# Where sixteen retention projection units stand among the RWKV-7 steps of a hybrid layer

## The reference

```python
def ab_mixer(h, pos, shift_prev, S_rwkv0, S_ret0, p, i):
    z = h @ p['ab_w_in'][i]
    za, zb = z[..., :A_SHIFT_COLS], z[..., A_SHIFT_COLS:]      # RWKV 1792, retention 2048 columns
    zs = za + (za_prev - za) * p['rwkv_mu'][i]
    ...                                                        # r, k, v, decay, a, gate, kk
    # per token: S = S*w - (S kk)(kk*a)^T + v k^T ;  o = S r
    o_a, S_rwkv = rwkv7_recurrence(r_h, decay, k_h, v_h, kk, a_h, S_rwkv0)
    o_a = (group_norm(o_a, ...) + sum(r_h * k_h * r_k) * v_h) * gate
    qr, kr, vr, gr = split(zb)                                 # 4 heads of 128 each
    qr = rotary(qr, pos); kr = rotary(kr, pos) * DK_B ** -0.5
    o_b, S_ret = retention_chunked(qr, kr, vr, S_ret0)
    o_b = group_norm(o_b, ...) * silu(gr)
    return concatenate([o_a, o_b], -1) @ p['ab_w_out'][i], ...
```

## Time and profile before

| what | value |
|---|---|
| median of three runs | 1522.76 us |
| the profiled execution | 1519.87 us, span 1518.1 us |
| TensorE matmul | 1421.7 us busy, 94% of the span |
| VectorE / ScalarE / GpSimd | 908.3 (60%) / 645.1 (42%) / 445.8 (29%) |
| mean granted TensorE clock | 0.97 |

### The profile page before, as it was taken

One profiled execution on the slowest core, in us unless ns is written; L12 is line 12 of the kernel. 1 busy time (PEld: TensorE's weight loads), 2 busy tenths in 40 slices (PEclk: granted clock), 3 DMA queues, 4 the chain that ended last, 5 costly groups with the idle time before them and its releaser, 6 DMA issues.

```text
span 1518.1 us, 30482 instructions
## 1 busy us (share of the span) xinstructions
PE 1421.7 (94%) x12028; PEld 1342.7 (88%) x12028; DVE 908.3 (60%) x1211; ACT 645.1 (42%) x975; POOL 445.8 (29%) x455
## 2 busy tenths in 40 slices
PE   7999999877998799999999999998998889999996
PEld 7999998866598589999999999987987769999996
DVE  4444456975464366555567776557777657655554
ACT  4333336533042434433443443366685444434333
POOL 3333132532221321112411114530006652111343
PEclk9999999999699799999999999999998999999998
DMA  7555543300053054555435555433434014455541
GB/s 277 166 165 186 171 130 98 109 6 30 22 177 98 21 180 139 164 158 186 164 118 164 159 163 182 164 92 119 134 133 153 30 71 167 140 165 165 187 156 51
DMA packets 50621, 203.37 MB, mean 134 GB/s; under 512 B 5696, under 2 KB 5696, under 8 KB 49760
## 3 DMA queue, kind: packets, MB, share of 16 engines
q1 hardware_dynamic: 46224, 181.03, 37.3%
q0 software_dynamic: 4016, 19.81, 3.6%
q10 hardware_dynamic: 288, 1.18, 0.2%
HBM read 192.17 MB, written 9.83 MB: 133 GB/s over the span
## 4 chain that ended last, share of the span: by engine, by line
PE 79%; DVE 11%; ACT 5%; issue 3%; POOL 1%; DMA 0%; ACTq 0%; POOLq 0%; DVEq 0%
PE gemm L2436 22%; PE gemm L2440 22%; PE gemm L2437 21%; DVE wlo L2388 3%; ACT whi L2383 2%; PE job L707 1%; PE gemm L2463 1%; PE job L739 1%; DVE M L1975 1%; PE gemm L513 1%; PE job L831 1%; PE job L1629 0%; PE job L1582 0%; PE job L1652 0%; PE job L849 0%
## 5 line engine op out<-in xcount | busy, mean ns | idle before, releaser
L2436 PE MATMUL gemm<-xhi,whi 128*128 128x290 f32 (+1 forms) x2040 | 619.9, 304 | 28.3 <-DVE wlo L2388 23.2
L2388 DVE TENSOR_TENSOR wlo<-raw,whi 128x1024 fp32r<-128x1024 f32 (+1 forms) x319 | 434.1, 1361 | 316.1 <-ACT whi L2383 313.8
L2383 ACT ACTIVATE whi<-raw 128x1024 fp32r<-128x1024 f32 (+1 forms) x319 | 358.5, 1124 | 607.3 <-PE gemm L2440 603.9
L2440 PE MATMUL gemm<-xlo,whi 128*128 128x290 f32 (+1 forms) x2040 | 610.5, 299 | 4.0 <-DVE xlo L400 4.0
L2437 PE MATMUL gemm<-xhi,wlo 128*128 128x290 f32 (+1 forms) x2040 | 607.6, 298 | 0.0
L2436 PEld LDWEIGHTS gemm<-xhi,whi 128*128 128x128 f32 x2040 | 389.5, 191 | 43.9 <-DVE wlo L2388 26.2
L2440 PEld LDWEIGHTS gemm<-xlo,whi 128*128 128x128 f32 x2040 | 388.4, 190 | 5.4 <-DVE xlo L400 4.7
L2437 PEld LDWEIGHTS gemm<-xhi,wlo 128*128 128x128 f32 x2040 | 389.6, 191 | 2.1
L2436 PE MATMUL gemm<-hhi,whi 128*128 128x288 f32 x704 | 209.6, 298 | 2.5 <-POOL hlo L2985 1.8
L2437 PE MATMUL gemm<-hhi,wlo 128*128 128x288 f32 x704 | 209.8, 298 | 0.0
L2440 PE MATMUL gemm<-hlo,whi 128*128 128x288 f32 x704 | 209.1, 297 | 0.0
(11 more groups left out here) (434 smaller groups left out, 1518.3 us busy)
## 6 DMA issues: line engine op xcount, KB each, us to landing
raw<-in_w_dram SPq DMA_DIRECT2D x255, 512.0 KB, 3.5
raw<-in_w_dram SPq DMA_DIRECT2D x64, 704.0 KB, 4.0
M<-in_ret_in_dram POOLq DMA_DIRECT2D x1, 2048.0 KB, 9.0
out_ret_s_dram<-M POOLq DMA_DIRECT2D x1, 2048.0 KB, 8.1
s_space<-in_gdn_in_dram POOLq DMA_DIRECT2D x4, 512.0 KB, 5.1
M<-in_gdn_in_dram POOLq DMA_DIRECT2D x4, 512.0 KB, 5.4
out_gdn_s_dram<-s_space POOLq DMA_DIRECT2D x4, 512.0 KB, 4.2
out_gdn_s_dram<-M POOLq DMA_DIRECT2D x4, 512.0 KB, 6.3
```

Of the source, the lines that this page charges most:

```text
L2383: nc.scalar.activation(whi[c % SPL][:, 0:w], raw[c % RAW][:, 0:w], ACT.Copy).then_inc(hi_ready, 1)
L2388: nc.vector.tensor_tensor(wlo[c % SPL][:, 0:w], raw[c % RAW][:, 0:w], whi[c % SPL][:, 0:w].bitcast(F32), ALU.subtract).then_inc(lo_ready, 1)
L2436: pe.matmul(bank[:, 0:w_], whi[s][:, w], hi[:, f0 + q, 0:w_], start=first, stop=False)
L2440: mm = pe.matmul(bank[:, 0:w_], whi[s][:, w], lo[:, f0 + q, 0:w_], start=False, stop=last)
```

## The change

The steps' code is moved into generators `between_units` on TensorE, ScalarE and VectorE. `stage("zb")` calls `next` on them after each unit, so each `yield` is a unit's place. With Pk for what TensorE runs behind unit k, the order is now:

- before unit 0: `bonus`, `nat`, both batches of `gram`; P0: `MV` of batch 0; P1: `MV` of batch 1, the inversion, `UW`, `OH`, `QG`;
- P2: the `chain`; P3: `OS`, `sgram`; P4: `sMV`, `sY`, `sP`; P5: `sXT`, `sX`; P6: `sU`; P7: `sO`, rotations 0 and 1; P8: `sS`;
- P9: `gnm`, rotations 2 and 3; P10: rotations 4 to 7, `gnv`; P11: nothing; P12: all three `rkn`, `rQ` 0; P13 to P15: as before.

On VectorE the body of unit 0 now holds `QG` of batch 0 and `UW` of batch 1, of unit 1 the second `QG` and the chain, of unit 2 `OS`, of unit 3 the sample masks, of unit 5 `sXT` and `sX`, of unit 6 `s_ub`, of unit 7 `sO` and two rotations, of unit 8 `sS`, of unit 9 `gnm` and two rotations, of unit 10 four rotations, of unit 11 `qx`, of unit 12 the three key drains and the group norm's scaling. ScalarE's follows the same numbers.

```diff
-            def keep_busy(n):
+            def keep_busy(n, j=0):
+                wait_count(pe, bank_free[j], TABLE["zb"][3][j])
                 for _ in range(n):
-                    pe.matmul(gemm[0][:, 0:SEQ], C("mean"), xsum[:, 0:SEQ], start=True, stop=True)
+                    pe.matmul(gemm[j][:, 0:SEQ], C("mean"), xsum[:, 0:SEQ], start=True, stop=True)
...
                 for j in range(2):
+                    yield
                     banks = [start(("MV", j, c)) for c in range(2)]
-                if j == 0:
-                    keep_busy(5)
...
-                keep_busy(2)
+                    if c < 3:
+                        keep_busy(2, 3)
+                yield
...
-            keep_busy(3)
+                yield
...
+            piece = between_units()
+            next(piece)
+            stage("zb", 1, lambda k: next(piece))
```

```diff
-        s_vb, s_ub = (m(A_BATCH + 4096 * i, 8, DB, 64, rows=slice(0, NS)) for i in range(2))
+        s_vb = m(B_S0, 8, DB, 64, rows=slice(0, NS))
+        s_ub_low = m(A_NAT, 6, DB, 64, rows=slice(0, NS))
+        s_ub_high = m(A_XK + 2048, 2, DB, 64, rows=slice(0, NS))
+        a_kts = m(A_XT + 4 * NS, 4, NS)
...
+                V.tensor_copy(a_kts, a_kt[:, :, SEQ:T])
...
+                for b in range(DB):
+                    nc.scalar.activation(s_ub_low[:, 0:3, b, :], s_u[:, 0:3, :], ACT.Copy, scale=selb[:, b:b + 1]
+                                         ).then_inc(sem("s_ub_low"), 1)
...
-            V.tensor_tensor(s_ub, bc(s_u, 2, DB), bc(bc(selb, 1, 8), 3, 64), ALU.mult).then_inc(sem("s_ub"), 1)
+                V.tensor_tensor(s_ub_low[:, 3:6, :, :], bc(s_u[:, 3:6, :], 2, DB), selb, ALU.mult
+                                ).then_inc(sem("s_ub_high"), 1)
+                V.tensor_tensor(s_ub_high, bc(s_u[:, 6:8, :], 2, DB), selb[:, 0:2, :, :], ALU.mult
+                                ).then_inc(sem("s_ub_high"), 1)
```

More of the change, by code:

```diff
@@ L517, in ab_tensor @@
[L517 to L551, removed]
@@ L641, in ab_tensor @@
-            J2 = slice(SEQ, T)
-            banks = [start(("sgram", e)) for e in range(2)]
-            for t in range(4):
-                for at, src in ((0, a_kk), (64, a_kt)):
-                    mms = [pe.matmul(banks[e][NROW, t * P + at:t * P + at + 64], src[half(e), t, J2],
-                                     kr[half(e), t, :, J2], start=True, stop=True) for e in range(2)]
-            for e in range(2):
-                fin(mms[e], ("sgram", e))
-            keep_busy(3)
-            bank = start(("sMV", 0))
@@ L698, in ab_tensor @@
-            fin(mm, ("sO", 0))
-            banks = []
-            for first in (True, False):
-                pe.wait_ge(sem("s_vb" if first else "s_ub"), 1)
-                for t in range(4):
-                    if first:
-                        banks.append(start(("sS", t)))
-                    for e in range(2):
-                        h = 2 * t + e
-                        mm = pe.matmul(banks[t][half(e), 0:512], a_nat[NROW, 2, 1 if first else 2, h * 64:(h + 1) * 64],
-                                       (s_vb if first else s_ub)[:, h, :, :], start=first, stop=not first)
-                    if not first:
-                        fin(mm, ("sS", t))
@@ L712, in ab_tensor @@
-            for k in (("OS", 1, 0), ("OS", 1, 1), ("sO", 0)):
-                pe.wait_ge(*out(k))
             def head_sums(key, src):
@@ L1145, in ab_vector @@
-            for j in range(2):
-                for c in range(2):
-                    dve.wait_ge(*out(("OH", j, c)))
-            for c in range(1, 4):
-                for e in range(2):
-                    key = ("chain", c, e)
-                    po = halves(e)[1]
-                    dve.wait_ge(*full(key))
-                    read(V.tensor_tensor(a_s[po, c - 1, :, :], jb(key, 256)[po].rearrange("p (t v) -> p t v", t=4),
-                                         a_h[po, :, c, :], ALU.add), key)
@@ L1181, in ab_vector @@
-            dve.wait_ge(*out(("sMV", 0)))
-            key = ("sX", 0)
-            dve.wait_ge(*full(key))
-            read(V.tensor_tensor(s_x, s_x, jb(key)[NROW].rearrange("p (h v) -> p h v", h=8), ALU.add), key)
-            dve.wait_ge(*out(("sU", 0)))
-            selb = C("selb", NROW)
-            V.tensor_tensor(s_ub, bc(s_u, 2, DB), bc(bc(selb, 1, 8), 3, 64), ALU.mult).then_inc(sem("s_ub"), 1)
-            for e in range(2):
-                dve.wait_ge(*out(("sP", e)))
-            key = ("sO", 0)
@@ L1394, in ab_pool, with cosines @@
                                 ).then_inc(sem("s0_faded"), 1)
+            def cosines(t0, t1):
+                for t in range(t0, t1):
+                    pool.wait_ge(*full(("rot", t)))
+                    G.tensor_tensor(b_z[:, t, :], b_z[:, t, :], C("cos"), ALU.mult).then_inc(sem("cosine"), 1)
+            cosines(0, 2)
             for t in range(4):
```

866 lines of the change are left out of this document (500 added, 366 removed).

## The result

| | median us | runs | ratio to the kernel before |
|---|---|---|---|
| before | 1523.82 | 4 (1520.61 to 1525.01) | 1 |
| changed | 1505.93 | 4 (1504.06 to 1508.88) | 0.9881 [0.9857, 0.9905] |

The change makes the kernel 1.2% faster, about 18 us. I forecast 1498 with 1488 to 1510: inside the range, 8 us above the point, close to the price of rival B (1507), though not by B's mechanism. The profiled execution took 1507.7 us, span 1505.9, 12.2 less than the span before.

What follows compares the result with a forecast made beforehand. Bound by a serial chain of small products and drains, filler in its holes, partly at half clock. 33.2 us go, 5.3 and 6.3 come; with smaller gains 24.3 us off the 1522.8 median, said as 1498, range 1488 to 1510.

Steps and rivals of the forecast that it cites:

- rival B: Sample steps: VectorE and ScalarE become the bound, nine steps each wait 1.3 us more, 14 instead of 5.3; 1507, chance 0.19.
- The walk through the queues: New, uncovered waits from splits and copies in the VectorE and ScalarE queues: together 5.3 us, bounds 2 and 14.
- (a): Behind the sample grams VectorE first splits and copies for the next units, so masks end late and sY waits: 1.1 us.
- (b): Rotations 2 and 3 use the banks of the first sums, drained behind a split and a copy: 1.4 us.
- (c): The four variance sums need the banks of rotations 4 to 7, which VectorE frees only gradually: 2.6 us.
- Idle and filler that I counted as gone: TensorE in the even layer: 11.9 us of waits and 7.2 us of filler matmuls disappear around the moved units.
- "issue" stalls: Two TensorE waits marked "issue", 1.9 us together, counted as gone since units put long matmuls between short ones.
- The clock that falls anew: Half clock around the sample state product and in L707, with the units after them: costs 6.3 us, bounds 0 and 12.
- ScalarE's early MV drains: MV drains lie beside unit 1 instead of before the first inversion's drains: a gain of about 1.2 us.
- A: Rival: the clock stays up through both thin stretches, a gain of 31.8 us; 1491, chance 0.22.
- C: Rival: drains set the chain, units only replace filler and waits return behind them; gain 8 us, 1515, chance 0.09.
- D: Rival: slower; clock falls in L668 and units get no full rate back until unit 13; 1533, chance 0.05.

Runs made afterwards that it cites:

- the control's run: The changed kernel repeated unedited as yardstick; median 1504.12 us (1497.80 to 1505.51), ratio 0.9879 to the kernel before; its profile is of the fastest run.
- the early scaling: Kernel before, with the first of four GpSimd query and key scalings in the odd layer made one step earlier: 1520.62 us, 0.9985.
- a kernel rearranged for it: Changed kernel with sample state product and update split across units, rotations 6 and 7 behind unit 11, first odd-layer GpSimd scaling earlier: 1495.43 us, 0.9812.

## Why the prediction held, and where it was off

**The walk through the queues held.** Unit 0 without a wait (0.0 us, said below 0.3); the first inversion product 2.1 us earlier (said 1.8); (a) 0.7 for a forecast of 1.1; (b) 1.35 for 1.4; (c) 1.38 + 0.54 + 0.21 = 2.1 for 2.6. Together 4.1 us for 5.1. Rival B's mechanism, nine steps with 1.3 us each, did not come. Idle and filler that I counted as gone are gone, except that the "issue" stalls only shrank: 3.0 us at L633 and L644, where there were 2.3 at L605 (the line that is L644 now), so 1.2 of 1.9 is gained.

**The mis-sized term is "The clock that falls anew", 6.3 us.** Each part against the same work at full clock, in the profiled run: the product took 5.94 us (4.49 in the control's run, where less of it is at half; I had left it at 5.16), 0.8 more than counted. Unit 5 took 6.0 instead of 3.45: 2.5 for my 1.7. The update took 11.3 instead of the 7.1 of 128 rows, 4.2 for my 2.7; it fell 2.7 us in, not 4. Unit 9 took 5.7 instead of 3.45, 2.3 for about 1.9. And a third stretch that I had not foreseen, at 446.9, where TensorE waits in the variance sums, costs about 1.1. Sum 10.9 us, 4.6 more than the term. That is within the bound of 12 that I gave.

The Trainium skill's sentence that "activity releases the throttle" (TensorE: Matmul & The Clock Gate, "Part 1: The HAM clock gate") was set against the earlier trace rows. The row was right to distrust it here: the engine is busy without a break in the update, yet the clock falls; with 128 rows it doesn't. A busy engine in the profile says nothing of its clock; the clock row does.

**The step that failed is one I did not have.** I wrote that I would be wrong if anything outside the even layer moved by over 2 us. It did, by 5.5 us in the profile: 4.1 by the collision and 1.4 ahead of it. I had taken the rest of the kernel as fixed because its code is. Which of the two outcomes a run takes goes with the TensorE clock ahead of the mask. Why the clock falls there in some runs, and why VectorE gets a joint between two GpSimd products when it starts late and none when it starts early, stays open. Whether the kernel before collides in some of its runs isn't known; its two profiles, one of them with the early scaling, have the later place.

**Terms without a row.** The 1.2 us that I added for ScalarE's early MV drains had no row behind them, and they did not come. VectorE's first step of the inversion, before and in the changed kernel:
```profile
333.47 2.84 DVE L1327 TENSOR_TENSOR M<-M,job 64x512 f32<-64x512 f32 x4 [6.87 <-PE job L862]
```
```profile
331.65 2.84 DVE L1405 TENSOR_TENSOR M<-M,job 64x512 f32<-64x512 f32 x4 [5.09 <-PE job L885]
```
It is 1.8 us earlier, which is what I had for the inversion's start alone. Two readings in my first paragraph are wrong as well, without a share in the sum: L707 is the update of the sample states and not the product with them, and up to 490 us the clock was low a fourth time, from 286.9 to 290.3 us, in both kernels' first profiles.

**The account** in the profiled run: 24.3 forecast; less 4.6 for the clock, 4.1 for the collision, 1.4 for what lies ahead of it in the same part, and 0.7 for issue stalls, plus 1.0 for shorter queue waits: 14.5. Measured 12.2. Of the last 2.3 us, which lie in the layer (20.0 by this account, 17.7 measured), 1.2 are the drains' term above; 1.1 are not placed. The control's fastest run stands at 1497.8 us, on the forecast's point, and that is luck: its clock falls later in both thin stretches and it has no collision, while the queue waits and the missing terms are the same.

**The other rivals.** A (1491) needs both falls away; a kernel rearranged for it reached 1495.4. C and D are out: idle and filler went, and units 6 to 8 run at 1.00 right behind the first fall. The chance of 0.92 for faster was in order.

## What to carry to other kernels

Units of dense work put into a chain of small products buy at least as much by the clock that they bring back as by the idle time that they fill: here the units among the sample steps were worth 10 us, of which idle and filler were 4 to 5. So lay them by the length of thin work between two of them, not by the waits, and split a thin step in two before adding filler. And when a change shifts everything behind it by some microseconds, look for places where VectorE and GpSimd both stream from on-chip memory: there unchanged code took 4 us more, and which runs did was set by a clock fall some microseconds ahead.

## What the runs showed of the hardware

- 32 matmul records with 32 rows and 512 columns, back to back, let the clock fall to 0.50 after 2.7 and 6 us in two runs of one kernel; 32 with 128 rows, of constants, kept it at 1.00. Two dense records of 0.3 us each ahead of every eight did not help; a unit of 3.4 us between two halves did.
- Nine runs of the same kernel spread by 11 us (1497.8 to 1508.9). Its two profiles, 9.9 us apart, differ by 4.2 us up to the last scores, with 10.2 us more at half clock, and by 5.3 behind them, 4.1 of it from the collision on. A difference of 3 us needs several runs of each, or several pairs.
- One VectorE multiplication of 128 x 256 took 0.41, 1.79 or 6.64 us at the same place of the same kernel, and both times it was long it ended some 0.3 us behind the end of a GpSimd product. Start 0.74 us behind the start of the first of these products went with the long one in seven profiles of seven, start 2.1 us behind it with the middle one in three of three.
